# Chunked RWKV recurrence on one core: triangles stored 64 columns wide, 64x64 products

## The reference

```python
def step(state, inp):
    r_t, w_t, k_t, v_t, a_t, b_t = inp
    sa = jnp.einsum('bhvk,bhk->bhv', state, a_t)
    state = (state * w_t[:, :, None, :]
             + sa[..., None] * b_t[:, :, None, :]
             + v_t[..., None] * k_t[:, :, None, :])
    y_t = jnp.einsum('bhvk,bhk->bhv', state, r_t)
    return state, y_t
```

## Time and profile before

| | us |
|---|---|
| median of 3 runs | 4466.98 (4465.72 to 4468.13) |
| the profiled execution's span | 4470.1 |
| stretch from 70 to 1190 us, where recurrence and band run together | 1120 |
| PE busy in that stretch | 1060.86 |
| DVE, ACT, POOL busy in that stretch | 499.49, 278.15, 177.94 |

### The profile page before, as it was taken

The page is one execution under the profiler, slowest core; times in us unless marked ns, Lnnn a source line. Parts: engine busy times, 40 slices in busy tenths (PEclk is TensorE's granted clock), DMA queues, the critical chain, the costliest instruction groups (busy, mean ns, idle before and its releaser), DMA issues.

```text
span 4470.1 us, 54722 instructions
## 1 busy us (share of the span) xinstructions
PE 4257.2 (95%) x23632; PEld 3420.8 (77%) x23632; DVE 1829.7 (41%) x3044; ACT 1335.7 (30%) x2354; POOL 1244.1 (28%) x634
## 2 busy tenths in 40 slices
PE   8999999999999999989999988999998999999998
PEld 4876867767599889867666766778777988888887
DVE  2444535354222224776310666123148432332343
ACT  3222222222223224356211345212246322121133
POOL 1211202112111345566122210224211433332244
PEclk9999999999999999999999999999998999999999
DMA  2101000000211112100011100120100121111110
GB/s 85 29 1 30 1 16 15 1 16 1 100 39 39 38 48 67 57 24 29 29 40 45 45 22 1 55 87 32 38 29 1 48 67 48 55 48 49 48 48 38
DMA packets 164961, 168.38 MB, mean 38 GB/s; under 512 B 8177, under 2 KB 152433, under 8 KB 164721
## 3 DMA queue, kind: packets, MB, share of 16 engines
q1 hardware_dynamic: 164720, 164.89, 11.6%
HBM read 156.48 MB, written 8.39 MB: 37 GB/s over the span
## 4 chain that ended last, share of the span: by engine, by line
PE 77%; DVE 13%; ACT 4%; POOL 3%; issue 2%; DMA 0%; POOLq 0%; SPq 0%; DVEq 0%; ACTq 0%
PE bank L625 15%; PE bank L627 14%; PE bank L626 14%; PE bank L590 8%; PE bank L1101 2%; PE bank L613 2%; PE bank L777 2%; PE bank L601 2%; PE bank L767 1%; PE bank L580 1%; PE bank L784 1%; PE bank L1116 1%; PE bank L888 1%; PE bank L874 1%; PE bank L1267 1%
## 5 line engine op out<-in xcount | busy, mean ns | idle before, releaser
L625 PE MATMUL bank<-XT_r,W_r 128*128 128x512 f32 x1744 | 700.9, 402 | 8.1 <-ACT BIG L1963 1.9
L626 PE MATMUL bank<-BIG_r,W_r 128*128 128x512 f32 x1624 | 632.5, 389 | 0.0
L3356 POOL TENSOR_TENSOR W_r<-W,W_r 128x2048 fp32r<-128x2048 f32 (+1 forms) x74 | 309.5, 4183 | 765.6 <-ACT W_r L1429 765.6
L627 PE MATMUL bank<-XT_r,W_r 128*128 128x512 f32 x1232 | 481.1, 390 | 0.0
L625 PE MATMUL bank<-W_r,BIG_r 128*128 128x256 f32 (+1 forms) x1280 | 418.0, 327 | 1.6 <-DVE H L2453 0.5
L590 PE MATMUL bank<-XT,W 128*128 128x512 f32 x928 | 412.3, 601 | 2.6 <-ACT BIG L1594 1.1
L625 PEld LDWEIGHTS bank<-XT_r,W_r 128*128 128x128 f32 x1744 | 328.2, 188 | 88.2 <-issue 14.2
L627 PE MATMUL bank<-W_r,BIG_r 128*128 128x256 f32 (+1 forms) x1152 | 380.4, 330 | 0.0
L626 PEld LDWEIGHTS bank<-BIG_r,W_r 128*128 128x128 f32 x1624 | 305.3, 188 | 72.0 <-issue 10.3
L590 PEld LDWEIGHTS bank<-XT,W 128*128 128x128 f32 x928 | 175.7, 193 | 213.3 <-issue 209.3
L627 PE MATMUL bank<-W_r,MIX_r 128*128 128x256 f32 x960 | 272.2, 284 | 0.0
(11 more groups left out here) (429 smaller groups left out, 8354.0 us busy)
## 6 DMA issues: line engine op xcount, KB each, us to landing
W<-w_in SPq DMA_DIRECT2D x29, 1024.0 KB, 5.3
W<-w_in_e SPq DMA_DIRECT2D x33, 512.0 KB, 6.4
MIX<-w_up SPq DMA_DIRECT2D x15, 1024.0 KB, 5.4
MIX<-w_down SPq DMA_DIRECT2D x15, 1024.0 KB, 4.8
W<-w_in_o SPq DMA_DIRECT2D x12, 1024.0 KB, 5.1
W<-w_in SPq DMA_DIRECT2D x17, 512.0 KB, 3.9
H<-x SPq DMA_DIRECT2D x16, 512.0 KB, 8.8
W<-w_out SPq DMA_DIRECT2D x7, 1024.0 KB, 5.1
```

What stands on the lines that cost most here:

```text
L625: E.matmul(b[:, 0:n], lh, rh, start=k == ks[0], stop=False)
L626: E.matmul(b[:, 0:n], lh, rl, start=False, stop=False)
L627: mm = E.matmul(b[:, 0:n], ll, rh, start=False, stop=k == ks[-1])
L3356: G.tensor_tensor(WLO[k % 2][:, 0:n], WSTAGE[k % 2][:, 0:n], WHI[k % 2][:, 0:n], ALU.subtract).then_inc(*s_split.mark("split", k))
```

## The change

The triangles are stored 64 columns wide: rows 0 to 63 of a tile hold the first chunk's, rows 64 to 127 the second's, and the zero halves are gone. A bank of 512 columns then holds 8 blocks `q` (4 tiles x 2 heads) instead of 4, so there are two groups for each pair instead of four. Every product of the factor is a 64x64x64 product, on array rows and columns 0 to 63 for the first chunk, 64 to 127 for the second; for `ym`, `f` and `g` all 8 of the first chunk are issued, then all 8 of the second (`PAIRS`). `wt` goes to two banks and ahead of `u0`; `yo` becomes eight 64x64 products; the chunk step waits for `u0` instead of `wt`. The 88 idle products ahead of `ym`, `f`, `x0`, `u0` and `us` are dropped from the table, `RW_ROUNDS` is 218, the scan over CS is made in two halves, and POOL copies the masks once into the narrow form. ACT, DVE and POOL keep their operations over 512 columns, and make half as many in the factor. The chunk products `us`, `ys` and `kv` are unchanged.

```diff
-        RW_ROUNDS, BAND_STEPS = 278, 192
+        RW_ROUNDS, BAND_STEPS = 218, 192
...
+                   [("RA", 2048), ("ROWS", HALF), ("LVL", 7 * 64), ("MASK2", 2 * 64), ("IDC", 64), ("WT0", 512),
+                    ("WT1", 512), ("W2", 512), ("ST", P), ("WC", 16), ("BON", 16)], WORK, WORK_N)
...
+        mask2 = rwv["MASK2"].rearrange("p (m n) -> p m n", n=64)
+        idc = rwv["IDC"]
+        LVL_WIDE = K[:, 0:7 * P].rearrange("p (m n) -> p m n", n=P)
+        MASK2_WIDE = R[:, 0:2 * P].rearrange("p (m n) -> p m n", n=P)
         BN, KN, AN = RAW[:, 1:SEQ + 1], T1, KK
         Am, AL, Fm, Gm, Ym = R[:, 0:HALF], R[:, HALF:], K[:, 0:HALF], K[:, HALF:], A[:, 0:HALF]
-        X0, UU = A[:, HALF:HALF + 256], SIG[:, 0:256]
+        X0, UU = Am, SIG[:, 0:HALF]
...
         def lv(i):
-            return lvl[:, i, :].unsqueeze(1).to_broadcast([P, 4, P])
+            return lvl[:, i, :].unsqueeze(1).to_broadcast([P, 8, 64])
+
+        def chunk_rows(ch):
+            return slice(ch * 64, ch * 64 + 64)
+
+        PAIRS = [(chunk_rows(ch), q) for ch in range(2) for q in range(8)]
+
+        def sq(q):
+            return slice(q * 64, q * 64 + 64)
...
+        idb = idc.unsqueeze(1).to_broadcast([P, 8, 64])
+        handed = [(SIG[:, HALF:SEQ], rwv["WT0"], by8(WS0[:, 3072:4096]), by8(WS1[:, 3072:4096])),
+                  (A[:, HALF:SEQ], rwv["WT1"], by8(CS), by8(EX))]
...
-        KEEP_UP.update({("rwkv", "ym", c, 0, 1): 4 for c in range(1, 4)})
...
-                {("rwkv", "us", *at): 2 for at in ((2, 4), (3, 4))}, {("rwkv", "bonus", 2): 3, ("rwkv", "bonus", 3): 4},
+                {("rwkv", "bonus", 2): 3, ("rwkv", "bonus", 3): 4},
...
-        def head_tiles(grp):
-            return [(2 * grp + i, h) for h in range(2) for i in range(2)]
+        def blocks(grp):
+
+            return [(4 * h + i, 4 * grp + i, i, h) for h in range(2) for i in range(4)]
...
-                for grp in range(4):
-                    if grp < 3:
-                        yield from weave(pe_chunks(c, grp), pe_factor(c, grp + 1))
-                    else:
-                        yield from pe_chunks(c, grp)
+                yield from weave(pe_chunks(c, 0), pe_factor(c, 1))
+                yield from pe_chunks(c, 1)
...
         def pe_factor(c, grp):
             U0, WT, AKT, ABT = handed[grp % 2]
-            tiles = head_tiles(grp)
-            for hf in range(2):
-                b = for_rw.open("rwkv", "am", c, grp, hf)
-                pe.wait_ge(*for_rw.free("rwkv", "am", c, grp, hf))
+            for h in range(2):
+                pr = slice(h * 64, h * 64 + 64)
+                b = for_rw.open("rwkv", "am", c, grp, h)
+                pe.wait_ge(*for_rw.free("rwkv", "am", c, grp, h))
                 pe.wait_ge(*done("rwkv", "ops", c))
-                for q, (t, h) in enumerate(tiles[2 * hf:2 * hf + 2]):
+                for i in range(4):
+                    t = 4 * grp + i
+                    for ch in range(2):
+                        rows = chunk_rows(ch)
+                        mm = E.matmul(b[rows, sq(i)], RA[pr, t, 0, rows], BT[pr, t * P + ch * 64:t * P + ch * 64 + 64],
+                                      start=True, stop=True)
+                mm.then_inc(*rw.pe.mark("rwkv", "am", c, grp, h))
+            for what, lhs in (("abt", BT), ("akt", KTL)):
+                for h in range(2):
                     pr = slice(h * 64, h * 64 + 64)
-                    mm = E.matmul(b[:, q * P:(q + 1) * P], RA[pr, t, 0, :], BT[pr, t * P:(t + 1) * P], start=True,
-                                  stop=True)
-                mm.then_inc(*rw.pe.mark("rwkv", "am", c, grp, hf))
-            for what, lhs in (("abt", BT), ("akt", KTL)):
...
-                    mm.then_inc(*rw.pe.mark("rwkv", what, c, grp, hf))
+                    b = for_rw.open("rwkv", what, c, grp, h)
+                    pe.wait_ge(*for_rw.free("rwkv", what, c, grp, h))
+                    for i in range(4):
+                        t = 4 * grp + i
+                        for ch in range(2):
+                            rows = chunk_rows(ch)
+                            mm = E.matmul(b[rows, i * P:(i + 1) * P], lhs[pr, t * P + ch * 64:t * P + ch * 64 + 64],
+                                          RA[pr, t, :, rows], start=True, stop=True)
+                    mm.then_inc(*rw.pe.mark("rwkv", what, c, grp, h))
...
                 pe.wait_ge(*for_rw.free("rwkv", "ym", c, grp, i))
-                pe_keep_up(b, "rwkv", "ym", c, grp, i)
                 pe.wait_ge(*done("rwkv", "al", c, grp, i))
                 pe.wait_ge(*done("rwkv", "fg", c, grp, i - 1))
-                for q in range(4):
-                    sl = slice(q * P, (q + 1) * P)
-                    mm = E.matmul(b[:, sl], AL[:, sl], Fm[:, sl], start=True, stop=True)
+                for rows, q in PAIRS:
+                    mm = E.matmul(b[rows, sq(q)], AL[rows, sq(q)], Fm[rows, sq(q)], start=True, stop=True)
                 mm.then_inc(*rw.pe.mark("rwkv", "ym", c, grp, i))
...
-                pe_keep_up(b, "rwkv", "f", c, grp, i)
                 pe.wait_ge(*done("ev", "rwkv", "ym", c, grp, i))
                 pe.wait_ge(*done("rwkv", "g0", c, grp))
-                for q in range(4):
-                    sl = slice(q * P, (q + 1) * P)
-                    mm = E.matmul(b[:, sl], Gm[:, sl], Ym[:, sl], start=True, stop=True)
+                for rows, q in PAIRS:
+                    mm = E.matmul(b[rows, sq(q)], Gm[rows, sq(q)], Ym[rows, sq(q)], start=True, stop=True)
...
-                        sl = slice(q * P, (q + 1) * P)
-                        mm = E.matmul(b[:, sl], Ym[:, sl], Gm[:, sl], start=True, stop=True)
+                    for rows, q in PAIRS:
+                        mm = E.matmul(b[rows, sq(q)], Ym[rows, sq(q)], Gm[rows, sq(q)], start=True, stop=True)
...
-            pe_keep_up(b, "rwkv", "x0", c, grp)
             pe.wait_ge(*done("rwkv", "fg", c, grp, 5))
...
+            for q, t, i, h in blocks(grp):
+                for ch in range(2):
+                    rows, at = chunk_rows(ch), i * P + h * 64
+                    mm = E.matmul(b[rows, at:at + 64], AKT[rows, q, 0, :], VN_R[rows, t * P + h * 64:t * P + h * 64 + 64],
+                                  start=True, stop=True)
             mm.then_inc(*rw.pe.mark("rwkv", "x0", c, grp))
             yield
+            for ch in range(2):
+                rows = chunk_rows(ch)
+                b = for_rw.open("rwkv", "wt", c, grp, ch)
+                pe.wait_ge(*for_rw.free("rwkv", "wt", c, grp, ch))
+                for q, t, i, h in blocks(grp):
+                    mm = E.matmul(b[h * 64:h * 64 + 64, sq(i)], AN[rows, t * P + h * 64:t * P + h * 64 + 64],
+                                  Fm[rows, sq(q)], start=True, stop=True)
+                mm.then_inc(*rw.pe.mark("rwkv", "wt", c, grp, ch))
             b = for_rw.open("rwkv", "u0", c, grp)
             pe.wait_ge(*for_rw.free("rwkv", "u0", c, grp))
-            pe_keep_up(b, "rwkv", "u0", c, grp)
             pe.wait_ge(*done("ev", "rwkv", "x0", c, grp))
-            for q, (t, h) in enumerate(tiles):
-                at = (t - 2 * grp) * P + h * 64
-                mm = E.matmul(b[:, at:at + 64], Fm[:, q * P:(q + 1) * P], X0[:, at:at + 64], start=True, stop=True)
+            for q, t, i, h in blocks(grp):
+                for ch in range(2):
+                    rows, at = chunk_rows(ch), i * P + h * 64
+                    mm = E.matmul(b[rows, at:at + 64], Fm[rows, sq(q)], X0[rows, at:at + 64], start=True, stop=True)
             mm.then_inc(*rw.pe.mark("rwkv", "u0", c, grp))
-            b = for_rw.open("rwkv", "wt", c, grp)
-            pe.wait_ge(*for_rw.free("rwkv", "wt", c, grp))
-            for i in range(2):
-                t = 2 * grp + i
-                for h in range(2):
-                    mm = E.matmul(b[:, (2 * i + h) * P:(2 * i + h + 1) * P], AN[:, t * P:(t + 1) * P],
-                                  Fm[:, (2 * h + i) * P:(2 * h + i + 1) * P], start=True, stop=True)
-            mm.then_inc(*rw.pe.mark("rwkv", "wt", c, grp))
...
-                    pe_keep_up(b, "rwkv", "us", c, n)
-                    pe.wait_ge(*done("ev", "rwkv", "wt", c, grp))
+                    pe.wait_ge(*done("ev", "rwkv", "u0", c, grp))
...
-                    hs = slice(h * 64, h * 64 + 64)
-                    E.matmul(b[:, hs], ABT[:, 2 * h + i, 1, :], ui[:, hs], start=True, stop=False)
-                    mm = E.matmul(b[:, hs], AKT[:, 2 * h + i, 1, :], VN_R[:, t * P + h * 64:t * P + h * 64 + 64],
-                                  start=False, stop=True)
+                    hs, q = slice(h * 64, h * 64 + 64), 4 * h + i
+                    vs = slice(t * P + h * 64, t * P + h * 64 + 64)
+                    for ch in range(2):
+                        rows = chunk_rows(ch)
+                        E.matmul(b[rows, hs], AKT[rows, q, 1, :], VN_R[rows, vs], start=True, stop=False)
+                    for ch in range(2):
```

(65 more changed lines are left out.)

52 lines of the change are left out of this document (18 added, 34 removed).

## The result

The changed kernel took **4546.84 us** (median of 4 runs, 4537.64 to 4594.58); the kernel before took 4466.67 in the same session (4465.72 to 4468.13). The ratio is **1.0197, 95% interval 1.0148 to 1.0246**: about 2% slower. Forecast were 4440 us and a range up to 4520. The time lies outside the range, on the other side of no change.

A forecast was written before the change was run, and what follows sets the result against it. PE, busy 95% of the span, was taken to bound the kernel. Terms 7 + 1.5 - 21 - 32 + 18 = -26.5 us took 4470.1 to 4443.6 profiled, a 4440 us median (0.6% faster); range 4345 to 4520.

The forecast's parts named there:

- a rival with 0.18: PE's clock in the recurrence falls to 0.93 under small products and lone chunk steps, costing 56 us: 4496 us; chance 0.18.
- The 64-wide products: The factor's 64x64 products on PE: 4864 records at 0.057 us instead of 2432 at 0.111, +7 us.
- The small pairs dear: Rival: a 64-wide load and product takes over 0.062 us, gain gone; 4528 us at 0.075, 4703 at 0.111; chance 0.12.
- am, abt, akt: These factor products on PE keep the same overlap, 53.3 to 55 us: +1.5 us, ends +18 and -27.
- Overlap of the two chunks: Chunks on different array rows overlap at operation boundaries and in x0, u0, yo: half of 42 us, -21; ends 0, -139.
- no overlap: Rival: the two chunks' products never overlap on PE since both halves write one bank: 4461 us; chance 0.15.
- Side by side throughout: Rival: both chunks' products run at once on PE throughout, overlap -139 instead of -21, about 4358 us; chance 0.17.
- Waits and idle products: PE's waits in the factor's chain and dropped idle products: half of 64 us goes, -32; ends -55 and -12.
- The sum's end of -12: Smaller saving on PE's waits and idle products, -12 us instead of -32, if chunk steps now alone lose their cover.
- Switches: PE entering and leaving 64x64 factor steps between 128x128 work: about 200 switches at 0.09 us, +18 us, 5 to 25.
- DVE, ACT, POOL at nothing: These engines lose about half their factor work, none bounds; split scans and extra mask copies on POOL were charged nothing.
- the work's own sum: All terms of the recurrence together, with the clock taken as unchanged: -26.5 us.

The follow-up runs named there:

- experiment 3: The changed kernel with four idle 128x128 products added ahead of each ym and each f: 4502.09 us.
- experiment 5: Experiment 1 plus four idle products ahead of us in the last 8 of 16 chunk steps of each pair: 4345.26 us, ratio 0.9756.
- Experiment 1: The changed kernel with ym, f and g taking the two chunks in turn instead of one after the other: 4375.00 us, ratio 0.9808.
- 8: The changed kernel, order not turned, with four idle products ahead of us in the lone chunk steps: 4551.28 us.
- 7: Experiment 1 with each product of ym, f and g issued twice, halves still in turn: 4458.14 us.
- 2: The kernel before with only its 88 idle products in the recurrence taken out: 4472.73 us, ratio 1.0028.

## Why the prediction was wrong

**The step that failed is the clock.** The sum took the granted clock of the stretch as unchanged at 0.98 and charged nothing for it; the clock was left to a rival with 0.18, sized at a mean of 0.93. It was 0.81. What that cost can be had from experiment 3, in which the factor's stretches run at the full clock with the same products in the same order. This table is mine, worked out from PE's records in the stage: the time from each record's start to the next, less the idle gaps, summed by kind.

```
us, in the stage       before   after   experiment 3   experiment 5
stage in all           1112.0  1171.1      1123.7          972.7
f, g                    136.6   165.5       121.4           75.6
ym                       78.6    96.7        73.3           44.4
abt, akt                 37.8    19.5        19.8           19.5
yo, wt, x0, u0           76.5    59.2        49.7           47.1
am                       10.0     5.7         6.3            5.7
sum of the factor       339.5   346.6       270.5          192.3
idle products            72.0    52.3       132.4           79.3
chunk steps us, ys, kv   82.8   103.2        94.2           81.5
other                   559.5   620.5       586.6          565.3
idle gaps                58.3    48.6        40.1           54.4
at the lower level       32.3   426.7       150.2           61.4
```

Before to after is +59 us. At the full clock the factor would have gone from 339.5 to 270.5, **-69**; the dropped idle products give -20 and the gaps -10. That makes -99, and so the clock cost 59 + 99 = **158 us**: 76 in the factor's own records (346.6 - 270.5), 81 in chunk steps and other work, whose products the change didn't touch. As a bound, (427 - 32) / 2 = 197 us would be lost if everything took twice as long at the lower level. The 158 is an estimate: some of the 81, up to about 10 us by the starts of PE's records, may be the new changes of array shape. And it has two parts. Experiment 1 leaves 181 us at the lower level, hardly any of it in the factor, and experiment 5 takes away 120 of them: the order of the halves accounts for the long stretches in the factor, the chunk steps that now stand alone for most of the rest. The rival had named both, products and lone steps, with a third of the price.

**Point by point, at the full clock.**

*The 64-wide products*, forecast 0.057 us a record: 0.0585 in a plain row, 0.054 with the seam. Right; the price read from the columns' slope held. The small pairs dear (from 0.062 on) is out. The Trainium skill, "TensorE: Matmul & The Clock Gate", section "LDWEIGHTS (loading the stationary operand)", has the load's time go by its columns alone; half the columns at half the time (0.0585 against 0.111) agrees.

*am, abt, akt*, forecast +1.5, ends +18 and -27: measured about -22 (47.8 to 26.1, in experiment 3). The column halves do run in parallel as well; I had put that at an end only.

*Overlap of the two chunks*, forecast -21 with 0.23 us at each boundary: at the boundaries the run-ahead is three records, 0.16 us, not four, 0.23; the term is a little smaller. x0, u0, wt and yo fell from 76.5 to 49.7 us; those that alternate run at 0.030, fully side by side, where I had counted half of the 29 us and then halved the sum again. The reason for halving again (one bank) didn't hold. The Trainium skill, "TensorEngine Tiling (Array Packing)", section "Gotcha 1: PSUM Pressure", was the ground of the rival "no overlap": in these runs two row halves that write different partitions of one bank do overlap, 0.030 against 0.054 us, so the measurement decides against it for this case. What happens when both write the same partitions of a bank no run here shows.

*Side by side throughout* (4358 us) named what the array can do, but not in this order. With the halves in turn it came: 4375, and 4345 with the lone steps covered. The change as made got a seam of three records for each operation.

*Waits and idle products*, forecast -32: -20 and -10. Right in sum, not in its parts. The factor's chain lost more wait than half, and the band's softmax took 19 us of it back, ahead of L617. The sum's end of -12, for lone steps that lose their cover, had this effect in view, though not this wait.

*Switches*, forecast +18: the extra time behind changes of array shape rose by 20 us in experiment 1 (24.1 to 44.6, my working from PE's starts), where the clock is near that of before. There are some 150 more changes (255 before, 408 in experiment 1) where I had counted 200, at about 0.1 us each. Right in sum.

*DVE, ACT, POOL at nothing*: right as a cost in the sum. Neither DVE nor POOL releases most of PE's idle time; ACT does, with about 32 of 48 us, 27 of them the band's softmax. Outside the stage the time moved by 7 us, with 163 and 145 us at the lower level there.

So the work's own sum would have come out better than forecast (-99 against -26.5), and one step charged at nothing turned it around. I had evidence in hand at one place: the earlier trace rows show the clock falling to 0.94 and 0.87 in the kernel before. I took 0.93 for the rival, milder than the worse of the two. But the change replaced every product of the factor by one on a quarter of the array, and no row of before showed such a stretch at any length; that called for a far wider bound than 0.93.

What the runs show of the cause: the clock falls for long stretches of the factor with the quarters one after the other (after, 8), though not in every factor; it holds there, but for 17 us, with the same products in turn (1), and throughout with full-array products between (3); and neither the length of an operation (7) nor the dropped idle products (2) nor the lone steps (8) is enough. So the order allows the fall and turning it prevents it. What starts a fall in one factor and not in the next, and what exactly the hardware counts, stays open. All four quarters at once was not tried for ym, f and g.

## What to carry to other kernels

When a matmul is cut down to a part of the array, price two things: the record (from a row at the full clock) and the clock, which can fall although PE is 96% busy; the row of granted clocks is then worth more than the busy shares. Put products of different row halves in turn in the instruction order, at most two by two: PE takes only about three records of the other half ahead. Here that one line of order was worth some 170 us, from 2% slower to 2% faster (ym, f and g alone went from 262 to 123 us). Where the rest of the clock is lost in thin stretches, a few idle products there pay (23 to 30 us), and between operations whose halves already take turns they don't (+49 us).

## What was not expected of the hardware

- With PE 96% busy and no wait over 0.9 us, the granted clock stayed at 1.2 GHz for 58 us (0.52 from 150 to 210 us) while records of one array quarter made up the factor; the same records in turn left it at 2.4 GHz, and so did, in the third pair, the same records in the same order.
- At the lower level a 64x64 pair of load and product takes 0.097 us against 0.054, and 0.054 against 0.030 where the halves alternate.
- PE starts matmuls out of program order: at all 32 seams of f and g records of the other row half begin among the last three of the half ahead of them, no earlier. From am to abt, whose column halves take turns as well, it is the last six.
- Two quarters on the diagonal write one bank at the same time without loss (0.030 us a record). The two column halves of one row half ran at 0.029 us a record too, and where am goes from one row half and bank to the other, closer still: its first 26 records come 0.023 us apart on the mean, and records of 128 columns (L761) 0.036:

```profile
143.89 0.80 PE L749 MATMUL bank<-BIG 64*64 64x64 f32 x26
...
144.65 2.43 PE L761 MATMUL bank<-BIG 64*64 64x128 f32 x61
```
